# Second MLP of a two-block transformer kernel: seven-product 2x2 blocks in ten of sixteen k-tile pairs of the down projection, and the up projection's matmuls grouped by shape

## What is computed

```python
def sq_relu_mlp(h, w_up, w_down):
    return jnp.square(jax.nn.relu(h @ w_up)) @ w_down        # 1024 -> 4096 -> 1024
...
        h = rms_norm_2(x, norm2_g[l])
        x = x + sq_relu_mlp(h, w_up[l], w_down[l])
```

## Time and profile before

| | us |
|---|---|
| median of 3 runs | 723.78 (723.59 to 724.34) |
| the profiled execution, its own time | 723.95 |
| its span in the trace | 722.2 |
| PE busy | 716.9 (99% of the span) |
| DVE, ACT, POOL busy | 488.2, 408.1, 170.5 |

### The profile page before, as it was taken

How to read it: one execution, slowest core, us unless ns; L and a number is a source line. 1 busy time by engine, 2 the same in 40 slices (tenths; PEclk the granted TensorE clock), 3 DMA queues, 4 the chain that set the end, 5 groups by cost and what they waited for, 6 DMA issues and landing times.

```text
span 722.2 us, 9237 instructions
## 1 busy us (share of the span) xinstructions
PE 716.9 (99%) x3514; PEld 596.2 (83%) x3514; DVE 488.2 (68%) x661; ACT 408.1 (57%) x530; POOL 170.5 (24%) x112
## 2 busy tenths in 40 slices
PE   9999999999999999999999999999999999999998
PEld 8777888888888888888888888888889888888886
DVE  6899999999987555555555356669765566654532
ACT  7646676655884454444445345479746676663330
POOL 1298999989300030000000000152000000000000
PEclk9999999999999999999999999999999999999999
DMA  9877446544566555666654664642364556456540
GB/s 319 261 219 231 145 146 205 183 154 161 175 229 237 169 181 176 187 193 195 194 178 158 212 204 129 230 174 67 109 204 159 178 181 211 176 197 211 174 146 29
DMA packets 83835, 131.59 MB, mean 182 GB/s; under 512 B 4064, under 2 KB 37032, under 8 KB 83792
## 3 DMA queue, kind: packets, MB, share of 16 engines
q1 hardware_dynamic: 83104, 130.28, 55.0%
q10 hardware_dynamic: 544, 0.53, 0.2%
q0 software_dynamic: 144, 0.20, 0.2%
HBM read 129.75 MB, written 1.25 MB: 181 GB/s over the span
## 4 chain that ended last, share of the span: by engine, by line
PE 96%; DVE 2%; POOL 1%; ACT 1%; issue 0%; ACTq 0%
PE acc L1770 24%; PE acc L1772 24%; PE acc L1771 24%; PE aux L1757 4%; PE aux L1431 3%; PE acc L1757 3%; PE acc L1763 2%; PE aux L1763 2%; PE aux L1474 1%; PE acc L1738 1%; PE acc L1746 1%; PE acc L1742 1%; PE aux L1492 1%; PE aux L1700 1%; PE acc L1760 1%; PE acc L1762 1%
## 5 line engine op out<-in xcount | busy, mean ns | idle before, releaser
L981 DVE TENSOR_TENSOR w_lo<-raw,w_hi 128x2048 fp32r<-128x2048 f32 x96 | 217.7, 2269 | 122.4 <-ACT w_hi L643 122.4
L643 ACT ACTIVATE w_hi<-raw 128x2048 fp32r<-128x2048 f32 (+1 forms) x115 | 218.0, 1899 | 136.0 <-PE acc L1772 110.6
L1770 PE MATMUL acc<-w_hi,h_both 128*128 128x512 f32 x488 | 195.0, 400 | 0.3 <-DVE tok L1051 0.3
L1772 PE MATMUL acc<-w_hi,h_both 128*128 128x512 f32 x488 | 190.6, 391 | 0.0
L1771 PE MATMUL acc<-w_lo,h_both 128*128 128x512 f32 x488 | 190.1, 390 | 0.0
L1770 PEld LDWEIGHTS acc<-w_hi,h_both 128*128 128x128 f32 x488 | 91.7, 188 | 20.0 <-issue 1.4
L1772 PEld LDWEIGHTS acc<-w_hi,h_both 128*128 128x128 f32 x488 | 91.6, 188 | 19.7
L1771 PEld LDWEIGHTS acc<-w_lo,h_both 128*128 128x128 f32 x488 | 91.8, 188 | 17.8
L625 POOL TENSOR_TENSOR w_lo<-raw,w_hi 128x2048 fp32r<-128x2048 f32 x21 | 97.8, 4668 | 1.4 <-ACT w_hi L643 1.4
L1040 DVE SCALAR_TENSOR_TENSOR aux<-glu_t,vec_t,aux 128x256 f32<-128x256 f32 x232 | 93.6, 482 | 0.0
L1770 PE MATMUL acc<-w_hi,m_hi 128*128 128x512 f32 x208 | 81.1, 390 | 0.0
(11 more groups left out here) (248 smaller groups left out, 900.8 us busy)
## 6 DMA issues: line engine op xcount, KB each, us to landing
raw<-w_in_dram SPq DMA_DIRECT2D x29, 1024.0 KB, 5.2
raw<-w_down_dram SPq DMA_DIRECT2D x26, 1024.0 KB, 5.0
raw<-w_gate_up_dram SPq DMA_DIRECT2D x44, 512.0 KB, 4.8
raw<-w_up_dram SPq DMA_DIRECT2D x16, 1024.0 KB, 5.5
raw<-w_out_dram SPq DMA_DIRECT2D x8, 1024.0 KB, 5.3
raw<-w_in_dram SPq DMA_DIRECT2D x12, 512.0 KB, 4.6
raw<-w_proj_attn_dram SPq DMA_DIRECT2D x4, 1024.0 KB, 5.0
raw<-w_proj_conv_dram SPq DMA_DIRECT2D x4, 1024.0 KB, 5.0
```

The costliest lines, as they stand in the source:

```text
L643: nc.scalar.activation(w_hi[:, u % SPLIT, 0:nk, :], raw[:, u % RAW, 0:nk, :], ACT.Copy)\
L981: nc.vector.tensor_tensor(w_lo[:, u % SPLIT, 0:nk, :], raw[:, u % RAW, 0:nk, :], f(w_hi[:, u % SPLIT, 0:nk, :]), ALU.subtract).then_inc(w_ ...
L1770: nc.tensor.matmul(o, x_h, w_hi[:, slot, j, :], start=begin_, stop=False)
L1772: mm = nc.tensor.matmul(o, x_l, w_hi[:, slot, j, :], start=False, stop=end_)
```

## The change

**Down projection.** It is now done 1024 columns at once. A group g is the k-tile pair (2g, 2g+1) by all 1024 columns: still 1 MB and one transfer. Seen as 2x2 blocks, with the two token tiles, the two k-tiles and the two column halves, a plain group takes 8 block products of 3 matmuls, 24 in all. Ten of the sixteen groups (`FAST`, 2 to 11) take 7 block products, 21 matmuls, by the Winograd variant of Strassen's form. The order of the groups is 0, 1, 12, 2 to 6, 13, 7 to 11, 14, 15 (`GROUPS`).

A fast group is two units. The "raw" unit has three block products with three of the four raw weight tiles (ACT splits 128x1536, POOL makes its low part). The "sum" unit has four block products with four sums of weight tiles. DVE makes the sums (`weight_sums`: 128x1024, 128x512, 128x512, each waiting for the one before), ACT their high part (2 of 128x1024), DVE their low part (2 of 128x1024). In plain groups of this stage POOL makes the low part (128x2048). The sums have two buffers, `w_hi` and `w_lo` a fourth cell, in the place of `h_both`. The first sums are put where `tok` and the first rows of `m_hi` lie, so they wait until PE is through with groups 0 and 1. When the last fast group is done, DVE combines four aux banks into the residual (ten instructions, 128x512 but for one) beside PE's last two plain groups.

**Activation sums.** For up chunks 1 to 5 (`FAST_UPS`) POOL adds four 128x256 instructions (`stationary_sums`), ACT and DVE one of 128x768 each for their two parts. `tok` has a second buffer.

**Up projection.** In chunks 1 to 7 the 16 matmuls of 512 columns of a unit come first and then its 16 of 256. PE waits for `w_lo` only between the two.

**Small ones.** Nine products of ones at the start in place of ten. DVE adds to `x_res` ahead of the split of unit 75. Some semaphores are merged; the three small tables of the start are waited for together.

In the diff, `split_low` with `nc.gpsimd` is POOL's, `weight_sums` and the loop over `SUMS` are DVE's, `parted` and the products are PE's.

```diff
-    out += [("res", 6 + i, w["w_down_2"], CW * i, None, list(range(0, FK2, UK)), FK2) for i in range(2)]
...
+    FAST = range(2, 12)
+    GROUPS = [0, 1, 12, *range(2, 7), 13, *range(7, 12), 14, 15]
+    FAST_UPS = range(1, 6)
+    late = []
+    for r, g in enumerate(GROUPS):
+        late += [("raw", g, NU + r), ("sum", g, NU + r)] if g in FAST else [("plain", g, NU + r)]
...
     def on_pool(u):
-        return 7 <= u <= 28 and u != 18
+        return 7 <= u <= 28 and u != 18 or u >= NU and late[u - NU][0] != "sum"
...
+        def cell_free(u):
+            p = u - NU
+            return u - SPLIT + 1 if p < 3 else NU if p == 3 else u - 3
...
+            def split_low(u):
+                pool.wait_ge(w_hi_ready, u + 1)
+                for src, part in zip(*unit_source(u)):
+                    nc.gpsimd.tensor_tensor(lo_cell(u)[:, part, :], src, f(hi_cell(u)[:, part, :]), ALU.subtract)\
+                        .then_inc(w_lo_pool, 1)
...
+            for u in range(NU, ALL):
+                if on_pool(u):
+                    split_low(u)
...
+            def weight_sums(n):
+                u = SUMS[n]
+                r = late[u - NU][2]
+                b12, b11, b22, b21 = (raw[:, r % RAW, k:k + 1, :] for k in range(4))
+                first_two, last_two = t_sums_hi[n % 2], t_sums_lo[n % 2]
+                dve.wait_ge(raw_in[r % RAW], raw_value[r])
+                if n < 2:
+                    dve.wait_ge(up_lo, 2 * FF2 // CW)
+                    dve.wait_ge(a_sum_lo, len(FAST_UPS))
+                    dve.wait_ge(unit_done, NU + 2)
+                else:
+                    dve.wait_ge(w_hi_ready, SUMS[n - 2] + 1)
+                    dve.wait_ge(w_lo_dve, low_no[SUMS[n - 2]])
+                nc.vector.tensor_tensor(first_two, raw[:, r % RAW, 1:3, :], again(raw[:, r % RAW, 0, :], 2), ALU.add)\
+                    .then_inc(t_made, 1)
+                dve.wait_ge(t_made, 3 * n + 1)
+                nc.vector.tensor_tensor(last_two[:, 0:1, :], first_two[:, 0:1, :], b22, ALU.add).then_inc(t_made, 1)
+                dve.wait_ge(t_made, 3 * n + 2)
+                nc.vector.tensor_tensor(last_two[:, 1:2, :], last_two[:, 0:1, :], b21, ALU.add).then_inc(t_made, 1)
...
+            weight_sums(0)
+            for n, u in enumerate(SUMS):
+                if n + 1 < len(SUMS):
+                    weight_sums(n + 1)
+                split_low(u)
...
+                if parted:
+                    for j in range(nk):
+                        for n in range(UK):
+                            nc.tensor.matmul(parts_of(i, n), w_hi[:, slot, j, P * n:P * (n + 1)],
+                                             h_both[:, :, k0 + j, :], start=is_first and j == 0, stop=False,
+                                             skip_group_check=True)
+                    pe.wait_ge(w_lo_dve, low_no[s])
+                    for j in range(nk):
+                        for n in range(UK):
+                            mm = nc.tensor.matmul(parts_of(i, n)[:, S:2 * S], w_lo[:, slot, j, P * n:P * (n + 1)],
+                                                  h_hi[:, k0 + j, :], start=False, stop=is_last and j == nk - 1,
+                                                  skip_group_check=True)
...
+                if kind == "raw":
+                    product(aux[:, 0, :], u, 0, *of_m(2 * g, 0), is_first, is_last)
+                    product(acc[:, 0, 0, :], u, 1, *of_sum(g, 2), False, False)
+                    mm = product(acc[:, 1, 0, :], u, 2, *of_m(2 * g + 1, 0), False, False)
+                if kind == "sum":
+                    product(aux[:, 1, :], u, 0, *of_sum(g, 0), is_first, is_last)
+                    product(aux[:, 3, :], u, 1, *of_m(2 * g, 1), is_first, is_last)
+                    product(aux[:, 2, :], u, 2, *of_sum(g, 1), is_first, is_last)
+                    mm = product(acc[:, 1, 1, :], u, 3, *of_m(2 * g + 1, 1), False, False)
...
-            idle_products(10)
+            idle_products(9)
...
+                if s == end["res", 3]:
+                    split_low(s - 1 + LEAD)
```

More of the change, by code:

```diff
@@ L278, in build @@
         raw_in = [sem(f"raw_in{i}") for i in range(RAW)]
[L279 removed]
+        x_loaded = [None, *(sem(f"x_loaded{g}") for g in range(1, UK))]
         piece_in = [sem(f"piece_in{k}") for k in range(PIECED * UK)]
@@ L494, in _ @@
                             sp.dma_start(tile[ps, :, ps], src).then_inc(lru_w_in, 16)
-            o_rows = out.rearrange("b (t p) d -> p (b t) d", p=P)
[L496 to L500, removed]
+            w, n = a["w_down_2"], D
+            for p, (kind, g, r) in enumerate(late):
+                if kind == "sum":
+                    continue
+                before = [NU + q for q, x in enumerate(late) if x[2] == r - RAW and x[0] != "sum"] or [r - RAW]
+                u = before[0]
+                sp.wait_ge(w_hi_ready, u + 1)
+                sp.wait_ge(w_lo_pool if on_pool(u) else w_lo_dve, low_no[u])
+                if u + 1 in SUMS:
+                    sp.wait_ge(t_made, 3 * SUMS.index(u + 1) + 3)
+                src = bass.AP(tensor=w.tensor, offset=w.offset + 2 * g * P * n, ap=[[n, P], [P * n, 2], [1, n]])
+                sp.dma_start(raw[:, r % RAW, :, :].rearrange("p (a b) c -> p a (b c)", a=2), src)\
+                    .then_inc(raw_in[r % RAW], 16)
+            o_rows = out.rearrange("b (t p) d -> p (b t) d", p=P)
+            for b, (n, t) in enumerate(BLOCKS):
+                sp.wait_ge(added, 12 + b + 1)
+                cols = slice(CW * n, CW * (n + 1))
+                sp.dma_start(o_rows[:, t, cols], x_res[:, t, cols]).then_inc(stored, 16)
             sp.wait_ge(stored, 16 * 2 * NT)
@@ L620, in _ @@
                     qk_power("k", 0)
[L621 to L626, removed]
+                if s + LEAD < NU and on_pool(s + LEAD):
+                    split_low(s + LEAD)
+                for i in FAST_UPS:
+                    if s == end["up", i]:
+                        stationary_sums(i)
                 if s in ended and s != K0 and ended[s][0] in ("q", "k") and ended[s][1] < 2:
                     qk_power(ended[s][0], ended[s][1])
+            for u in range(NU, ALL):
+                if on_pool(u):
+                    split_low(u)
         @block.scalar
@@ L746, in _ @@
                 for i in range(FF2 // CW):
[L747 to L753, removed]
+                    if s == end["up", i] + 1 and i not in FAST_UPS:
+                        keep_up(i)
                 for hd in range(H):
@@ L973, in _ @@
                         nc.scalar.activation(y_hi[:, n, :], aux[:, n, 0:S], ACT.Copy).then_inc(o2_hi, 1)
+                for i in FAST_UPS:
+                    if s == end["up", i] + 1:
+                        keep_up(i)
+            for u in range(NU + LEAD + 2, ALL):
+                split_high(u)
         @block.vector
@@ L1146, in _ @@
                 for i in range(FF2 // CW):
[L1147 to L1153 removed]
+                    if s == end["up", i] + 1 and i not in FAST_UPS:
+                        up_low(i)
                 if s == LN:
@@ L1714, in _ @@
                     pe.wait_ge(added, 12)
+                parted = chunks[c][0] == "up" and chunks[c][1] > 0
                 if s >= PIECED:
@@ L1747, in _ @@
                                                   stop=is_last and j == nk - 1)
-                    for n in range(UK) if chunks[c][0] == "up" else ():
-                        i = chunks[c][1]
+                    for n in range(UK) if chunks[c][:2] == ("up", 0) else ():
                         o = channels_of(c, n)
@@ L1777, in _, with product, of_m @@
                 after(s)
+            def product(o, u, j, a_h, a_l, begin_, end_):
+                w_h, w_l = hi_cell(u)[:, j, :], lo_cell(u)[:, j, :]
+                nc.tensor.matmul(o, a_h, w_h, start=begin_, stop=False, skip_group_check=True)
+                nc.tensor.matmul(o, a_h, w_l, start=False, stop=False, skip_group_check=True)
+                return nc.tensor.matmul(o, a_l, w_h, start=False, stop=end_, skip_group_check=True)
+            def of_m(kt, t):
+                return m_hi[:, kt, P * t:P * (t + 1)], m_lo[:, kt, P * t:P * (t + 1)]
```

276 lines of the change are left out of this document (196 added, 80 removed).

## The result

The changed kernel takes 751.80 us (median of 4 runs, 751.12 to 752.75) against 723.81 (723.59 to 724.34) for the kernel before on the same chip: ratio 1.0385, 95% interval 1.0372 to 1.0398. It is 28.0 us slower. The profiled execution has a span of 751.0 us and a time of its own of 752.75.

What follows compares the result with a forecast made beforehand. PE bounded the kernel before; in the changed down projection DVE and POOL taking turns would decide. 722.2 + 24.5 - 1.4 - 0.2 - 0.15 = 745.0 us of span, forecast as 746.5 us, range 740 to 757.

Steps and rivals of the forecast that it cites:

- Matmuls removed: Down projection: 354 matmuls, 30 fewer than 384, at 0.2267 us each, take 6.8 us of PE work away.
- Up projection by shape: Up projection: grouping 512- and 256-column matmuls saves 0.0067 us per pair; 1.4 us off, between 0 and 1.5.
- Start and end of the first MLP: First MLP: one product of ones fewer saves 0.2 us, and PE's wait for `x_res` goes, 0.15 us.
- DVE and POOL exclude each other: Down projection: DVE and POOL passes cannot overlap, so times add: 8.6 us per fast group against PE's 4.76.
- Rival 1: Down projection: no exclusion, DVE's chain decides alone with 1.6 us of waits; faster, 716.8 us; chance 0.13.
- A handover: Down projection: the blocked engine ends 1.07, not 1.21 us behind the other; 0.15 saved some 22 times, 3.3 off.
- The layout of the stage: Down projection: timeline of DVE and POOL passes in turn, giving a stage of 111.5 us, 24.5 more than before.
- E: The down projection's start, from which the forecast counted its times in us.
- the way: Down projection: what passes of DVE and POOL can use only one at a time; 48.0 plus 36.5 us of use.
- The upper bound: Whole kernel: about 753 us, with no saving in handovers (3.3 more) and ACT and PE waiting in turn (3 more).
- Waits of PE: Down projection: PE stands some 3.5 us before most sum units, about 8 ahead of group 13's, some 30 in all.
- Rival 2: Down projection: PE's clock falls to 1.2 GHz in the waits, about 10 us more, 757 us; chance 0.13.

Runs made afterwards that it cites:

- the version with seven fast groups: Changed kernel with seven fast groups in place of ten, spread between plain ones, all the down projection's low parts on DVE: 717.39 us, ratio 0.9910 to the kernel before.
- the two runs where it fell into the tail: Changed kernel with 104 zero-adding products in PE's waits, 751.74 us; seven fast groups, low parts on DVE but plain tiles' on POOL, 729.97 us.

## Why the prediction was right

It named 746.5 us in a range of 740 to 757; 751.8 lies in it, 5.3 above the number. By its steps:

- **Matmuls removed.** 354 in the stage, at 0.2267 us where the clock is full (a plain unit of 24 takes 5.44). Right, and seen whole in the version with seven fast groups.
- **Up projection by shape.** Forecast 1.4 us off; 1.22 in the changed kernel, 1.21 alone. Right; of the 0.0067 us per pair some 0.0054 were the change of shape.
- **Start and end of the first MLP.** Forecast 0.35 together; the up stage begins 0.31 sooner, the first real matmul at 5.11 in place of 5.39.
- **DVE and POOL exclude each other.** Shown by three runs: with POOL writing only, DVE's passes are 1.22 and 0.69 us beside a busy POOL and 31.9 us go; with POOL idle and its work on DVE 24.4 go; with part of it back on POOL 12.6 return (in the version with seven; 2.5 of them are the half clock). Rival 1 (716.8) fell. Without the lock its number would have been near: the run with writes only takes 719.94, 3.1 more, with 3.4 us of waits where rival 1 had 1.6. A handover saves 0.15 us as forecast (1.08 behind POOL's end against 1.23).
- **The layout of the stage** is where the 5.3 us are, all in terms that were too small. Forecast: way clear of the early passes at E + 11.9 and the ninth sum unit's low part done at E + 93.1. In the trace the first weight sum starts at 645.04, E + 14.8, and that low part ends at 729.01, E + 98.8. So 2.9 us are at the start. "POOL holds the way until E + 11.9" took it that POOL waited for ACT's copy of the first raw tile; it had three passes in a row, from E + 0.8 to E + 13.6: the low parts of groups 1 and 12, which the prediction left out of this stretch, ahead of that of group 2. DVE's low parts of the last activations (the row at 637.07) were held until the last of these ended, and the sums stand behind them. Another 2.2 are the stretch in which nobody used the way. The upper bound held a term for that ("may leave ACT and PE waiting in turn", 3 us), but its cause is the half clock. Together 5.1 of the 5.7 us by which the stage was longer than the forecast 111.5. The rest lies in the handovers: from the first sum to that low part 16 passes were held up, nine of DVE's and seven of POOL's, and not 22, which gives some 2.4 us off in place of 3.3. That the way was used for 81.7 us (83.97 less 2.24) against 81.2 forecast is thus in part luck: passes queued on DVE save a little, which the forecast had in its lower bound and not in its sum; the tail of 81 matmuls was as forecast (729.16 to 747.40, 18.2 against 18.4). The median is missed by a little less, 5.3, since the changed kernel's profiled execution is 0.95 above its median.
- **Waits of PE.** Forecast "some 30 us in all", 3.5 before most sum units and 8 before the one ahead of group 13: 26.2 between the starts, beside the 11 us of slow matmuls, 8.05 ahead of that one, 0.7 to 4.9 before others, none before three. The waits alone are near the forecast (with the slow matmuls they make 37), the even spacing was wrong.
- **Rival 2, PE's clock falls in the waits.** Its condition came true and its price did not. The clock fell in the waits of 7.4, 3.7, 8.1 and 4.9 us, and with it full to the end the kernel is 1.6 us faster, not 10. The step that failed in it: it let the half clock add 0.7 us in each of ten groups, but DVE and POOL keep their own pace whatever PE's is, the clock was half for 31 us and not throughout, and PE's slow units mostly ran into time in which it would have stood. The Trainium skill (TensorE: Matmul & The Clock Gate, "HAM oscillation — how this bites in real kernels") tells of waits between bursts that bring the half clock back: the trace agrees for the long ones here, while the 1.7 us before six sum units, in the kernel with all low parts on DVE, left it full. What the slow time costs is a second question: almost nothing in the changed kernel, where waits hid it, and all of it in the two runs where it fell into the tail (1.6 and 2.5 us).

## What to carry to other kernels

Before giving POOL work "to relieve DVE", look at the operands: where POOL reads SBUF and DVE has two SBUF inputs, their times add, and POOL's slower pass is dearer than the same pass on DVE. Removing products from a bound PE pays only up to the point where the helpers' time per product saved fits under PE's: with ten fast groups and part of the helpers' work on POOL the stage lost 30.3 us, with ten and all of it on DVE 4.7, and with seven, mostly spread out and all on DVE, it won 4.7. A fallen clock behind a wait is a symptom first; ask what PE would have waited for at full clock before pricing it. Where other waits follow, it may cost nothing; in the tail it costs in full.

## What the runs showed of the hardware that was not expected

A fill on POOL (1.81 us for 2048 columns, 1.38 for 1536) does not hold up DVE in this stage (passes of 128x1024 stay at 1.22 us), though it writes the whole tile. Passes of DVE queued behind one another start up to 0.1 us before the record of the one ahead ends, so that 1.22 + 0.69 + 0.69 + 1.75 + 1.22 + 1.22 = 6.8 us of records take 6.53. And a matmul of 512 columns takes 0.228 us from start to start in a run of one shape in the up projection, where the moving operand is two pieces of 256 columns (552.31 to 555.96 for 16 of them), against 0.2267 in the down projection: the pieces cost next to nothing. One thing more stands in the trace and was not looked into: DVE does not always get its turn behind one pass of POOL's. The first low part issued at 637.07 stood through the ends of two, at 640.29 and 643.81.

```profile
552.31 3.82 PE L1907 MATMUL aux<-h_both,w_hi 128*128 128x512 f32 x16
555.96 0.76 PE L1913 MATMUL aux<-h_both,w_lo 128*128 128x256 f32 x5
```
